# Sparse experts for 32 tokens: indexed row transfers and VectorE beside a dense expert stage of 224 tokens

## The reference

```python
q = (xt @ wq).reshape(T, PEER_HEADS, 2, PEER_HALF)
s = jnp.einsum('thpc,phnc->thpn', q, subkeys)
top_s, top_i = lax.top_k(s, PEER_TOPK)                     # 16 of 128 keys, for 8 heads, 2 halves
best_s, best_pos = lax.top_k(cand_s, PEER_TOPK)            # 16 of the 256 pairs
expert = ...                                               # 8 heads x 16 = 128 experts a token
g = jax.nn.softmax(best_s, axis=-1)
hid = gelu(einsum('td,thkd->thk', xb, u[eb]))
out = einsum('thk,thkd->td', g * hid, v[eb])
```

## Time and profile before

| | |
|---|---|
| median of 3 runs | 2158.81 us (2156.8 to 2161.62) |
| the profiled execution | span 2156.3 us; it is an execution of its own, whose time from outside is not given apart |
| TensorE busy | 2138.4 us, 99% |
| VectorE, ScalarE, GpSimd busy | 1546.2, 1207.9, 703.6 us |
| moved by DMA | 377.13 MB, mean 175 GB/s |

### The profile page before, as it was taken

The page is one execution under the profiler, slowest core; times in us unless marked ns, Lnnn a source line. Parts: engine busy times, 40 slices in busy tenths (PEclk is TensorE's granted clock), DMA queues, the critical chain, the costliest instruction groups (busy, mean ns, idle before and its releaser), DMA issues.

```text
span 2156.3 us, 39034 instructions
## 1 busy us (share of the span) xinstructions
PE 2138.4 (99%) x13024; PEld 1891.9 (88%) x13024; DVE 1546.2 (72%) x2748; ACT 1207.9 (56%) x1988; POOL 703.6 (33%) x342
## 2 busy tenths in 40 slices
PE   8999999999999999999999999999999999999999
PEld 7777889999999988888877778899999999888887
DVE  5867869977777666666568678699767786666665
ACT  5855455477877533333367554555778785333332
POOL 1300016877777500000023000178777774000000
PEclk9999999999999999999999999999999999999999
DMA  6444554554444555555654445545545445555654
GB/s 239 155 142 144 195 172 151 181 181 157 164 161 161 177 192 191 191 193 194 195 199 156 140 148 194 166 156 183 172 163 165 163 160 180 191 193 191 191 194 155
DMA packets 103756, 377.13 MB, mean 175 GB/s; under 512 B 11760, under 2 KB 11760, under 8 KB 103152
## 3 DMA queue, kind: packets, MB, share of 16 engines
q1 hardware_dynamic: 102528, 371.24, 52.6%
q10 hardware_dynamic: 1136, 4.79, 0.6%
HBM read 374.94 MB, written 1.05 MB: 174 GB/s over the span
## 4 chain that ended last, share of the span: by engine, by line
PE 94%; DVE 3%; ACT 2%; issue 1%; DMA 0%; POOL 0%; ACTq 0%; SPq 0%; POOLq 0%; DVEq 0%
PE ps L517 28%; PE ps L519 28%; PE ps L518 28%; PE ps L869 3%; PE ps L525 3%; PE ps L527 1%; PE ps L536 1%; DVE w_lo L1299 1%; PE ps L652 1%; PE ps L830 1%; ACT w_hi L969 1%; PE ps L732 0%; PE ps L611 0%; DVE arena L1401 0%; DVE keep_lo L1422 0%
## 5 line engine op out<-in xcount | busy, mean ns | idle before, releaser
L1168 ACT ACTIVATE w_hi<-raw 128x1024 fp32r<-128x1024 f32 x512 | 523.5, 1054 | 438.6 <-PE ps L519 437.9
L502 POOL TENSOR_TENSOR w_lo<-raw,w_hi 128x1024 fp32r<-128x1024 f32 x264 | 634.1, 2417 | 267.9 <-ACT w_hi L1168 267.9
L517 PE MATMUL ps<-hT,w_hi 128*128 128x256 f32 x2048 | 580.1, 283 | 0.0
L518 PE MATMUL ps<-hT,w_hi 128*128 128x256 f32 x2048 | 579.6, 283 | 0.0
L519 PE MATMUL ps<-hT,w_lo 128*128 128x256 f32 x2048 | 579.6, 283 | 0.0
L517 PE MATMUL ps<-w_hi,wgt_hi 128*128 128x512 f32 x1024 | 398.5, 389 | 0.0
L518 PE MATMUL ps<-w_lo,wgt_hi 128*128 128x512 f32 x1024 | 398.4, 389 | 0.0
L519 PE MATMUL ps<-w_hi,wgt_lo 128*128 128x512 f32 x1024 | 398.4, 389 | 0.0
L518 PEld LDWEIGHTS ps<-hT,w_hi 128*128 128x128 f32 x2048 | 393.2, 192 | 0.0
L519 PEld LDWEIGHTS ps<-hT,w_lo 128*128 128x128 f32 x2048 | 393.2, 192 | 0.0
L517 PEld LDWEIGHTS ps<-hT,w_hi 128*128 128x128 f32 x2048 | 393.2, 192 | 0.0
(11 more groups left out here) (202 smaller groups left out, 2885.1 us busy)
## 6 DMA issues: line engine op xcount, KB each, us to landing
raw<-in_w_u SPq DMA_DIRECT2D x256, 512.0 KB, 3.4
raw<-in_w_v SPq DMA_DIRECT2D x256, 512.0 KB, 3.7
raw<-in_stream SPq DMA_DIRECT2D x192, 512.0 KB, 3.5
arena<-in_bias ACTq DMA_DIRECT2D x2, 1024.0 KB, 5.6
arena<-in_subk ACTq DMA_DIRECT2D x2, 1024.0 KB, 5.0
x<-in_x SPq DMA_DIRECT2D x4, 256.0 KB, 4.3
out<-x SPq DMA_DIRECT2D x4, 256.0 KB, 2.2
arena<-in_params ACTq DMA_DIRECT2D x2, 283.5 KB, 3.6
```

The source lines that it names most:

```text
L502: nc.gpsimd.tensor_tensor(w_lo[:, i, :], raw[:, i, :], w_hi[:, i, :].bitcast(F), ALU.subtract).then_inc(early_ready.sem, 1)
L517: mm(out_, left[0], right[0], start=start, stop=False, skip_group_check=group)
L518: mm(out_, left[0], right[1], start=False, stop=False, skip_group_check=group)
L1168: f(w_hi[:, slot, :], raw[:, slot, :], ACT.Copy).then_inc(hi_ready.sem, 1)
```

## The change

Tokens 0 to 31 leave the dense stage. `SPARSE = 32`, `DENSE = 224`.

- *Dense part.* The up products have 224 moving columns, G is 128 x 224 a key, there are 56 groups, spread evenly over the fill pairs by `DOUBLED` (5 for 4 pairs). In the down stage the table v is the stationary operand, in eight pieces of 128 columns; the moving one is the weights of 224 tokens, hi and lo side by side: `expert_chunk`, one product of 448 columns with w_hi, one of 224 with w_lo. The output stands transposed, features in partitions, in all 8 banks. Of the subtractions in the down stage, those of the odd pairs move from VectorE to GpSimd.
- *Sparse part.* Each of the 128 partitions holds one of 32 tokens and a quarter of its 128 experts, so that a gather q fetches one row for each partition (128 rows of 4 KB, an indirect DMA that GpSimd issues). 32 gathers take rows of u, and VectorE multiplies each with the token's normed x and sums (`dot`, one for a fill pair from pair 6 on). ScalarE applies gelu to the 32 sums. 32 gathers take rows of v, and VectorE adds each, times its weight, into `xs` (`add_rows`, one for a down pair from pair 4 on). `add_sparse` adds the four quarters to x at pair 36. The rows land in a ring of three. VectorE works out the row numbers in `rows()`, after the choice for tile 0, and spreads the gate weights in `shares()`, after the choice for tile 1. ScalarE issues four copies of x's 32 rows and a load of the gains.
- *End.* ScalarE copies the lo half out of PSUM, VectorE adds (`turn`), TensorE transposes back (`out_transposes`), VectorE adds to x (`add_experts`).
- The loops of the fill and down stages are written out on GpSimd and VectorE, the fill pairs on TensorE.

Left out below: the new signals, `groups_of`, the gelu shapes, the loads' counters, the host's two new arrays.

```diff
-N_POOL = N_EARLY + 2 * FILL + SLOTS
+N_U = N_EARLY + 2 * FILL
+N_POOL = N_U + PAIRS + 2
 N_DVE = N_LAYER - N_POOL
-N_V = N_STREAM - SLOTS
+SPARSE = 32
+DENSE = T - SPARSE
+PARTS = P // SPARSE
+GROUPS = DENSE // 4
+RING = 4 * SPARSE // 32 - 1
+GATHERS = 2 * SPARSE
+FIRST_DOT, FIRST_SUM = 6, 4
...
-        wgt_hi, wgt_lo = overlay(("wgt_hi", [P, 2, 512], FR), ("wgt_lo", [P, 2, 512], FR))
+        (wgt,) = overlay(("wgt", [P, 2, 2, 2, DENSE], FR))
...
-        G = view(0, KEYS, T)
+        G = view(0, KEYS, DENSE)
+        spare = [view(KEYS * DENSE + D * i, D) for i in range(RING + 1)]
+        xs, ring = spare[2], spare[:2] + spare[3:]
+        v_low = view(0, 8, DENSE)
...
+        outT = view(8 * DENSE, 8, T)
...
+                def gather(q):
+                    table, s = (u_rows, q) if q < SPARSE else (w_v.rearrange("l p k n -> (l p k) n"), q - SPARSE)
+                    if q >= RING:
+                        pool.wait_ge(g_taken.sem, g_taken.at(layer, q - RING + 1))
+                        pool.sem_inc(seen_pool, 1)
+                    nc.gpsimd.indirect_dma_start(
+                        out=ring[q % RING], out_offset=None, in_=table,
+                        in_offset=bass.IndirectOffsetOnAxis(ap=row_of[:, s:s + 1], axis=0)
+                        ).then_inc(gathered[q % RING].sem, 16)
...
+                pool.wait_ge(rows_known.sem, rows_known.at(layer, 1))
+                pool.sem_inc(seen_pool, 1)
+                asked = RING
+                for q in range(RING):
+                    gather(q)
+                for pair in range(FILL):
+                    for e in range(2):
+                        n = N_EARLY + 2 * pair + e
+                        split_e(n, n % SLOTS)
+                    while asked <= min(pair - FIRST_DOT, SPARSE + RING - 1):
+                        gather(asked)
+                        asked += 1
...
+                for pair in range(PAIRS):
+                    if pair == 0 or pair % 2:
+                        for e in range(2):
+                            split_e(N_U + 2 * pair + e, 2 * (pair % 2) + e)
+                    while asked <= min(SPARSE + pair - FIRST_SUM + 2, GATHERS - 1):
+                        gather(asked)
+                        asked += 1
...
-                        last = product(ps[:, 2 + k, e * T:(e + 1) * T],
+                        last = product(ps[:, 2 + k, e * DENSE:(e + 1) * DENSE],
                                        [w[:, 2 * k + e, kc * P:(kc + 1) * P] for w in (w_hi, w_lo)],
-                                       [h[:, kc, :] for h in (hT_hi, hT_lo)], start=(kc == 0), stop=(kc == KC - 1))
+                                       [h[:, kc, SPARSE:T] for h in (hT_hi, hT_lo)],
+                                       start=(kc == 0), stop=(kc == KC - 1))
...
+                def expert_chunk(k, e, c, first=False):
+                    dims = slice(c * P, (c + 1) * P)
+                    mm(ps[:, c, 0:2 * DENSE], w_hi[:, 2 * k + e, dims], wgt[:, k, e, :, :].rearrange("p a b -> p (a b)"),
+                       start=first, stop=False, skip_group_check=True)
+                    return mm(ps[:, c, 0:DENSE], w_lo[:, 2 * k + e, dims], wgt[:, k, e, 0, :],
+                              start=False, stop=False, skip_group_check=True)
...
+                def out_transposes(n):
+                    pe.wait_ge(outT_ready.sem, outT_ready.at(layer, n + 1))
+                    for c in (2 * n, 2 * n + 1):
+                        last = transposes(ps[:, c, :], outT[:, c, :], 2)
+                    last.then_inc(outT_mm.sem, 1)
                 for n in range(4):
...
+                    for c in (2 * n, 2 * n + 1):
+                        for e in range(2):
+                            last = expert_chunk(1, e, c)
                     last.then_inc((v_part if n < 3 else v_mm).sem, 1)
+                    if n == 2:
+                        out_transposes(0)
+                for n in range(1, 4):
+                    out_transposes(n)
+                    if n == 2 and layer + 1 < LAYERS:
+                        x_there(1, layer + 1)
+                        norm_transposes(lambda n: x_there(n, layer + 1), (0, 1))
...
+                def rows(layer=layer):
+                    own.one(v.scalar_tensor_tensor(out=expert, in0=rt_tok[0:SPARSE, 0, 0, :], scalar=float(KEYS),
+                                                   in1=rt_tok[0:SPARSE, 0, 1, :], op0=ALU.mult, op1=ALU.add
+                                                   ).then_inc(dve_chain, 1))
+                    dve.wait_ge(xs_loaded.sem, xs_loaded.at(layer, 16 * PARTS))
+                    dve.wait_ge(gain_loaded.sem, gain_loaded.at(layer, 16))
+                    own.one(v.tensor_tensor(xs, xs, ring[0], ALU.mult).then_inc(dve_chain, 1))
+                    for j in range(PARTS):
+                        own.one(v.tensor_copy(scale_of[j * SPARSE:(j + 1) * SPARSE, :], rstd[0:SPARSE, 0:1]).then_inc(dve_chain, 1))
+                    for j in range(PARTS):
+                        last = v.tensor_scalar(row_of[j * SPARSE:(j + 1) * SPARSE, :],
+                                               expert[:, j * SPARSE:(j + 1) * SPARSE], float(layer * KEYS * KEYS), None, ALU.add)
+                    last.then_inc(rows_known.sem, 1)
+                def shares():
+                    dve.wait_ge(rt_ready.sem, rt_ready.at(layer, 1))
+                    for j in range(PARTS):
+                        own.one(v.tensor_copy(share[j * SPARSE:(j + 1) * SPARSE, :],
+                                              rt_tok[0:SPARSE, 0, 2, j * SPARSE:(j + 1) * SPARSE]).then_inc(dve_chain, 1))
...
+                    rows_ = ring[s % RING]
+                    v.tensor_tensor_reduce(out=rows_, in0=rows_, in1=xs, scale=1.0, scalar=0.0, op0=ALU.mult, op1=ALU.add,
+                                           accum_out=hid[:, s:s + 1]).then_inc(g_taken.sem, 1)
+                def share_out():
+                    dve.wait_ge(hid_gelu.sem, hid_gelu.at(layer, 1))
+                    own.one(v.tensor_tensor(hid, hid, share, ALU.mult).then_inc(dve_chain, 1))
+                    dve.wait_ge(dve_chain, own.n)
+                def add_rows(s):
+                    q = SPARSE + s
+                    landed(q)
+                    rows_ = ring[q % RING]
+                    if s == 0:
+                        last = v.tensor_scalar(xs, rows_, hid[:, 0:1], None, ALU.mult)
+                    else:
+                        dve.wait_ge(g_taken.sem, g_taken.at(layer, q))
+                        last = v.scalar_tensor_tensor(out=xs, in0=rows_, scalar=hid[:, s:s + 1], in1=xs,
+                                                      op0=ALU.mult, op1=ALU.add)
+                    last.then_inc(g_taken.sem, 1)
...
+                def add_sparse():
+                    dve.wait_ge(g_taken.sem, g_taken.at(layer, GATHERS))
+                    own.one(v.tensor_tensor(x[0:SPARSE, 0, :], x[0:SPARSE, 0, :], xs[0:SPARSE, :], ALU.add).then_inc(dve_chain, 1))
+                    for j in range(1, PARTS):
+                        own.one(v.tensor_copy(ring[j - 1][0:SPARSE, :], xs[j * SPARSE:(j + 1) * SPARSE, :]).then_inc(dve_chain, 1))
+                    for j in range(1, PARTS):
+                        dve.wait_ge(dve_chain, own.n)
+                        own.one(v.tensor_tensor(x[0:SPARSE, 0, :], x[0:SPARSE, 0, :], ring[j - 1][0:SPARSE, :], ALU.add
+                                                ).then_inc(dve_chain, 1))
...
+                    if 0 <= u - FIRST_DOT < SPARSE:
+                        dot(u - FIRST_DOT)
                 dve.wait_ge(fill_used.sem, fill_used.at(layer, FILL))
                 dve.sem_inc(seen_dve, 1)
+                for p in range(2, PAIRS):
+                    weigh(p)
+                    if p % 2 == 0:
                         for e in range(2):
...
+                            split_e(2 * p + e, e)
+                    q = p - FIRST_SUM
+                    if q == 0:
+                        share_out()
+                    if 0 <= q < SPARSE:
+                        add_rows(q)
+                    if q == SPARSE:
+                        add_sparse()
+                dve.wait_ge(v_part.sem, v_part.at(layer, 1))
+                dve.sem_inc(seen_dve, 1)
+                own.one(v.memset(outT[:, :, 0:SPARSE], 0.0).then_inc(dve_chain, 1))
+                dve.wait_ge(dve_chain, own.n)
...
+                def turn(n):
+                    dve.wait_ge(v_lows.sem, v_lows.at(layer, n + 1))
+                    v.tensor_tensor(outT[:, 2 * n:2 * n + 2, SPARSE:T], ps[:, 2 * n:2 * n + 2, 0:DENSE],
+                                    v_low[:, 2 * n:2 * n + 2, :], ALU.add).then_inc(outT_ready.sem, 1)
+                def add_experts(half):
+                    dve.wait_ge(outT_mm.sem, outT_mm.at(layer, 2 * half + 2))
+                    for t in range(TT):
+                        tile = x_tile(2 * half + t).rearrange("p (a b) -> p a b", a=4)
```

(25 more changed lines are left out.)

199 lines of the change are left out of this document (116 added, 83 removed).

## The result

The changed kernel takes **2256.8 us** (median of 4 runs, 2253.72 to 2258.22) against 2160.22 for the kernel before in the same comparison: ratio 1.044, 95% interval 1.042 to 1.046. The forecast was 2200, in the range and on the right side, but +41 of it against +97 measured.

A forecast was written before the change was run, and what follows sets the result against it. TensorE, 99% busy, was taken as the bound, with VectorE and GpSimd close behind in the early and fill stages. 2 x (7 + 4.5 + 4) + 10 = +41 on 2156.3 gave 2197, forecast as 2200 us, range 2080 to 2320.

The forecast's parts named there:

- the fill: Fill stage, 44 pairs: GpSimd becomes the bound at 6.8 us a pair with dots; +4.5 us a layer (-24 to +43).
- GpSimd runs 74% of the time, half of 2.4 on average, 0.9: VectorE 6.2: Fill stage: each dot waits 0.9 us on average for GpSimd, bringing VectorE to 6.2 us a pair.
- the gather takes its turn too: Rival, fill and down stages: GpSimd's 1.2 us of asking also excludes VectorE's two-input operations; 2315 us, chance 0.15.
- Early +7: Early stage: rows() delays the route by 8 us and TensorE stands; +7 us a layer (3 to 13).
- Down +4: Down stage: turns cost +11 with add_rows, -15 without, add_sparse +8; +4 us a layer (-29 to +30).
- Ends +10: Ends of the layers: TensorE stands 6.5 us between layers, and 3.5 us are added at the end; +10 for both.
- TensorE's gain: Products of 224 columns take 0.110 us instead of 0.120 for 256; 130 us in all, alone giving 2026.
- narrow products gain nothing: Rival, products of 224 columns: they stay at 0.120 us, adding 22 us in both layers; 2222 us, chance 0.12.
- the turns stay hidden: Rival, fill and down stages: VectorE and GpSimd keep enough slack that TensorE sets the pace; 2075 us, chance 0.25.

The follow-up runs named there:

- e8: Changed kernel with each dot's second operand read from PSUM instead of the copy of x, all transfers kept: 2168.5 us.
- e10: Changed kernel reordered: late row numbers, VectorE making the down stage's subtractions, 16 dots at every second fill pair, 16 in the down stage: 2102.4 us.
- e12: Changed kernel reordered: late row numbers, VectorE making the down stage's subtractions, 10 dots at every fourth fill pair, 22 in the down stage: 2099.5 us.
- e7: Changed kernel with VectorE making all table subtractions from the down stage's third pair on, GpSimd only issuing transfers there: 2204.5 us.
- e9: Changed kernel with row numbers and GpSimd's request for them moved behind the fill's first pairs, ScalarE's tile 1 exponents one pair later: 2243.9 us.
- e1: Changed kernel without the 32 tokens' own sparse path, dense experts still at 224 tokens: 2079.4 us.

## Why the prediction was right on the side and wrong by half

- **The term that failed is the fill: +4.5 a layer forecast, +27.4 measured in layer 1 and +24.4 in layer 2.** The step: "GpSimd runs 74% of the time, half of 2.4 on average, 0.9: VectorE 6.2." The dot's own 1.2 was right (1.22 in e8 and in the down stages of e10 and e12). The wait was 2.0, not 0.9, because the starts aren't random: all 64 dots began while a subtraction ran (not 74%), and 28 of them in the last 0.3 us of the first of two, so that they waited for the second as well. VectorE: 4.1 + 3.2 = 7.3 a pair; from the first dot (508.70) to the 32nd (740.08) it is 7.46. The sum named GpSimd (6.8) as the bound, and the windows show VectorE at 50 of 50 and GpSimd at 43 to 44. 32 x (7.46 - 6.8) = 21 of the 23 us a layer that are missing. In e8 the same stretch has 6.06 a pair.
- The gather, taken at 1.2, costs 0.97 by itself (e8) and 1.70 beside the dots. The rival *the gather takes its turn too* (2315) is out: the gather is drawn out by VectorE, but VectorE's subtractions beside it keep their 1.22 (e7). That 2257 lies between 2200 and 2315 doesn't speak for it.
- **Early +7, measured +10.3.** The 8 us for rows() were 9.8 (390.8 to 400.6). Not foreseen: ScalarE's exponents in front of the rounding, 7.3 us of standing ahead of the route. TensorE stood 13.7 us in two pieces, near the forecast 15, but the clock then cost about 4.2 us where 1 was taken. e9 shows the term to be one of order.
- **Down +4, measured +3.6** to the last down product, 348.9 before and 352.5 after. Its working holds: two pairs take 11.24 us with `add_rows` (11.6 forecast) and 10.03 without (9.92), and `add_sparse` costs 9.8 (8). That the sum comes so near is in part luck, as one part was taken too high and two too low. By e7, take the turns away and 26 us go.
- **Ends +10, measured about +11**: 7.6 against 0.6 us at the layers' border, and 7.5 from the last down product to the end (2246.67 to 2254.2) against 3.8. Forecast 6.5 and 3.5.
- **TensorE's gain.** Products of 224 columns start 0.1115 us apart (438.16, 438.27, 438.38), between my 0.110 and the 0.120 of the rival *narrow products gain nothing*, which is out: e1 is 83 us under the 2162.1 of its comparison, with the longer ends already in it. The Trainium skill (TensorE: Matmul & The Clock Gate, section LDWEIGHTS) would have left them at 0.120 by my working; the measurement decides.
- The rival *the turns stay hidden* (2075) failed for this order of work. e12 comes within 25 us of it with the same computation.
- Layer 2 adds some 45 us (2254.2 - 1134.7 against 2156.3 - 1081.8), with the same terms. Of the +53 at layer 1's end, 4.6 were there before the early stage; kernels alike up to that point start it anywhere between 332.6 and 337.1, so I name no cause.

## What to carry to other kernels

Before putting work on an idle-looking engine, ask where its operands lie. Beside GpSimd's subtractions an operation of VectorE with two inputs in SBUF cost its own time plus 1.0 to 2.5 us; one with an input in PSUM cost its own time. The wait depends on where in GpSimd's work it starts, and a late start in the first of two operations is the worst. A neighbour's busy share doesn't give the wait: read one such operation in the timeline against the neighbour's rows, or time a one-column version of it. And if two engines exclude each other, giving all of the work to the faster one (e7) can beat sharing it.
